# First attention of a streaming encoder step: stacked key and query parts for the scores

## The reference, cut to what matters

```python
k_sel = k_all[idx]; v_sel = v_all[idx]           # idx = top_k(indexer score)
logit = einsum('bqgrd,bqkgd->bqgrk', qg, k_sel) * HEAD_DIM ** -0.5
p = softmax(where(valid, logit, -inf))
o = einsum('bqgrk,bqkgd->bqgrd', p, v_sel)       # 16 query heads, 4 key heads, 64 wide
```

## Time and profile before

| | us |
|---|---|
| median of 3 runs | 1539.61 (1539.01 to 1540.18) |
| profiled execution, span from first to last instruction | 1537.2 |
| profiled execution, time of its own | not listed beside the span |
| first attention, from its first to its last turn of pairs | 183.2 to 281.8 |

### The profile page before, as it was taken

One profiled execution on the slowest core, in us unless ns is written; L12 is line 12 of the kernel. 1 busy time (PEld: TensorE's weight loads), 2 busy tenths in 40 slices (PEclk: granted clock), 3 DMA queues, 4 the chain that ended last, 5 costly groups with the idle time before them and its releaser, 6 DMA issues.

```text
span 1537.2 us, 29298 instructions
## 1 busy us (share of the span) xinstructions
PE 1496.9 (97%) x11509; PEld 1374.7 (89%) x11509; DVE 1057.4 (69%) x2025; ACT 634.3 (41%) x1265; POOL 580.0 (38%) x346
## 2 busy tenths in 40 slices
PE   5999999999999999999999999999999999999998
PEld 2768966899999999999888888887999999999998
DVE  1559866668887778877634444457997877688753
ACT  3434366444552145532533333335254541355423
POOL 1234841124662056642222222231227640366421
PEclk8999999999999999999999999999999999999999
DMA  9874510232244433443264444442542355343521
GB/s 333 269 264 150 140 37 2 72 108 69 83 129 141 156 89 104 121 141 99 51 191 127 127 126 126 126 127 71 168 120 56 83 160 184 83 110 83 152 83 62
DMA packets 244455, 189.23 MB, mean 123 GB/s; under 512 B 12888, under 2 KB 228608, under 8 KB 240112
## 3 DMA queue, kind: packets, MB, share of 16 engines
q1 hardware_dynamic: 231232, 178.61, 38.9%
q10 hardware_dynamic: 13104, 8.97, 1.8%
HBM read 175.44 MB, written 8.50 MB: 120 GB/s over the span
## 4 chain that ended last, share of the span: by engine, by line
PE 86%; DVE 5%; ACT 3%; issue 2%; DMA 2%; POOL 1%; SPq 0%; ACTq 0%; POOLq 0%; DVEq 0%
PE lin L858 40%; PE lin L1430 26%; PE lin L875 5%; PE S L1199 2%; PE O L993 1%; PE O L1321 1%; PE O L1252 1%; DVE acc_out L2644 1%; PE S L1274 1%; ACT act_hi L1655 1%; PE T L1232 1%; DMA ada_raw<-in_w_ada 1%; PE S L1118 1%; PE S L1062 1%; PE T L1289 1%
## 5 line engine op out<-in xcount | busy, mean ns | idle before, releaser
L2137 POOL TENSOR_TENSOR w_lo<-w_raw,w_hi 128x1024 fp32r<-128x1024 f32 (+3 forms) x68 | 168.2, 2475 | 407.7 <-ACT w_hi L1602 407.7
L2228 POOL TENSOR_TENSOR w_lo<-ada_raw,w_hi 128x512 fp32r<-128x512 f32 x114 | 156.5, 1375 | 242.8 <-ACT w_hi L1903 242.8
L1602 ACT ACTIVATE w_hi<-w_raw 128x1024 fp32r<-128x1024 f32 (+2 forms) x110 | 125.1, 1139 | 225.5 <-PE lin L858 212.3
L858 PE MATMUL lin<-act_hi,w_hi 128*128 128x288 f32 (+1 forms) x1088 | 164.6, 302 | 4.9 <-ACT act_hi L1634 2.0
L858 PE MATMUL lin<-act_hi,w_lo 128*128 128x288 f32 (+1 forms) x1088 | 167.3, 300 | 0.2
L858 PEld LDWEIGHTS lin<-act_hi,w_hi 128*128 128x128 f32 (+1 forms) x1088 | 149.5, 190 | 15.1 <-issue 10.3
L858 PE MATMUL lin<-act_lo,w_hi 128*128 128x288 f32 (+1 forms) x1088 | 162.1, 298 | 0.0
L858 PEld LDWEIGHTS lin<-act_hi,w_lo 128*128 128x128 f32 (+1 forms) x1088 | 150.0, 188 | 7.4 <-issue 6.7
L858 PEld LDWEIGHTS lin<-act_lo,w_hi 128*128 128x128 f32 (+1 forms) x1088 | 149.6, 188 | 3.4 <-issue 2.9
L2228 POOL TENSOR_TENSOR w_lo<-s_tmp,w_hi 128x512 fp32r<-128x512 f32 x76 | 129.2, 1718 | 15.0 <-ACT w_hi L1906 14.7
L1430 PE MATMUL lin<-act_hi,w_hi 128*128 128x288 f32 x608 | 105.5, 296 | 0.7 <-DVE Z L2801 0.7
(11 more groups left out here) (347 smaller groups left out, 3023.5 us busy)
## 6 DMA issues: line engine op xcount, KB each, us to landing
ada_raw<-in_w_ffn_in SPq DMA_DIRECT2D x76, 512.0 KB, 5.2
w_raw<-in_w_ffn_out SPq DMA_DIRECT2D x32, 704.0 KB, 5.0
ada_raw<-in_w_ada SPq DMA_DIRECT2D x20, 1024.0 KB, 7.8
ada_raw<-in_w_ada SPq DMA_DIRECT2D x32, 512.0 KB, 5.1
w_raw<-in_w_in_b SPq DMA_DIRECT2D x32, 512.0 KB, 4.2
w_raw<-in_w_in_a SPq DMA_DIRECT2D x16, 512.0 KB, 5.9
ada_qo<-in_w_ada SPq DMA_DIRECT2D x8, 1024.0 KB, 7.3
ada_raw<-in_w_ada_final SPq DMA_DIRECT2D x16, 512.0 KB, 5.6
```

What stands on the lines that cost most here:

```text
L858: last = nc.tensor.matmul(lin_u(u)[0:m, tok], w, (lo if p == 2 else hi)[:, at(t) if at else t, tok], start=(p == 0 and t == 0), stop=(p == ...
L1602: A(w_hi[:, u % 2, 0:n], w_raw[:, u % 2, 0:n], ACT.Copy).then_inc(whi_done, 1)
L2137: TT(w_lo[:, u % 2, 0:n], w_raw[:, u % 2, 0:n], w_hi[:, u % 2, 0:n].bitcast(F32), ALU.subtract)\
L2228: TT(ring(w_lo, q), raw, ring(w_hi, q).bitcast(F32), ALU.subtract).then_inc(ws_lo_p, 1)
```

## The change

Keys and queries of the first attention get a high and a low part in fp32r. `kT4` becomes fp32r and holds, for each key head, the high part on one half of the partitions and the low part on the other. The queries of a pair lie in `q_hi` (two buffers) and in `q_lo0` or `q_lo1`, for each head on all 128 partitions: both halves the same. A score is then two products of full height, `q_hi` and `q_lo` against the stacked key parts, added in PSUM. The samples of both heads lie side by side, so that one pair of products gives their scores and DVE takes their maximum in one operation. The score products of pair p read none of `qo`.

- ACT: `k_high` in place of `k_dup` (as many copies); `q_high`, three copies for each pair: pairs 0 and 1 between the projections' copies, pair p + 2 after the exponentials that ACT computes at k = 2 of pair p.
- POOL: `k_low` after `split_lo(U_V + 1)` and after `split_lo(U_Q + 2)`; `q_lows` of pairs 3 to 7 after `split_pair` of pairs 0 to 4.
- DVE: `q_lows` of pairs 0, 1 and 2, within the last top-k rounds, after the second `max_unit` and at n = 3; `cache_keys` makes both parts of the cached keys.
- SP: `q_double`, four DMAs for each pair, from the half of the partitions that has a head to the other half; pairs 2 to 7 stand in its queue one behind the other after the swap for the last queries, and the loads of the first sums come after them. `q_hi` and `q_lo0` share their place with `ada_raw`, whose first loads for sums therefore wait for the last score unit.
- PE: before the scores of a pair it waits for the four DMAs in place of the rotation.

```diff
+        q_hi = sb("q_hi", [P, 2, 2 * TOK], F32R, scope=s)
+        q_lo0 = sb("q_lo0", [P, 2 * TOK], F32R, scope=s)
...
-        kT4 = sb("kT4", [P, NG, NK], scope=a)
+        kT4 = sb("kT4", [P, NG, NK], F32R, scope=a)
...
+        Q_PARTS = [(0, 0, TOK, 0), (1, NP_, TOK, TOK), (1, 0, NP_, TOK + NS)]
+        def q_tile(e, k):
+            c = k * P if e == 0 else TOK + NS + k * P
+            return slice(c, c + P)
...
-                    sp.wait_ge(ada_used, 3 * KT)
+                    sp.wait_ge(s_done, 4 * PAIRS)
...
+            def q_double(pair):
+                sp.wait_ge(qhi_done, pair + 1)
+                sp.wait_ge(qlo_done, pair + 1)
+                for buf in (q_hi[:, pair % 2, :], q_low(pair)[:, :]):
+                    for e in range(2):
+                        own, other = slice(64 * e, 64 * e + 64), slice(64 - 64 * e, P - 64 * e)
+                        cols = slice(e * TOK, (e + 1) * TOK)
+                        sp.dma_start(buf[other, cols].bitcast(F32), buf[own, cols].bitcast(F32))\
+                          .then_inc(qdup_in[pair % 2], 16)
...
+                if j == 6:
+                    q_double(0)
...
+            def last_queries(m):
+                if m < 3:
+                    rope_swap(U_Q + PAIRS - 3 + m)
+                if m == 0:
+                    q_double(1)
+                if m == 2:
+                    for pair in range(2, PAIRS):
+                        q_double(pair)
...
-                    pe.wait_ge(rope_done, rope_of(U_Q + n // 4) + 1)
+                    pe.wait_ge(qdup_in[n // 4 % 2], 64 * (n // 8 + 1))
             def sa_unit(n):
                 k, pair, bank = n % 4, n // 4, (S, S2)[n % 2]
-                groups = [(0, P, k * P, 0, (k + 1) * P, 384 if k == 0 else 0)]
+                halves = (q_hi[:, pair % 2, :], q_low(pair)[:, :])
+                nk, col = (k + 1) * P, 384 if k == 0 else 0
+                for e in range(2):
+                    for j, q in enumerate(halves):
+                        last = nc.tensor.matmul(bank[:, e, col:col + nk], q[:, q_tile(e, k)],
+                                                kT4[:, pair // 2, 0:nk], start=(j == 0), stop=(j == 1))
                 if k == 0:
-                    groups.append((1, NS, NP_, NP_, PAST + NS, 0))
-                for sample, rows, tok, key, nk, col in groups:
-                    for e in range(2):
-                        r = slice(64 * e, 64 * e + 64)
-                        out = bank[64 * e:64 * e + 64] if sample else bank[0:P]
-                        last = nc.tensor.matmul(out[:, e, col:col + nk], qo[r, pair, tok:tok + rows],
-                                                kT4[r, pair // 2, key:key + nk],
-                                                start=True, stop=True)
+                    for j, q in enumerate(halves):
+                        last = nc.tensor.matmul(bank[:, 0, 0:PAST + NS], q[:, NP_:NP_ + 2 * NS],
+                                                kT4[:, pair // 2, NP_:NK], start=(j == 0), stop=(j == 1))
                 last.then_inc(s_done, 1)
...
-            pe.wait_ge(kdup_done, 2)
+            pe.wait_ge(khi_done, 8)
+            pe.wait_ge(klo_done, 4)
...
+            def k_high(j):
                 act.wait_ge(rope_done, rope_of(U_K + j) + 1)
-                for e in range(2):
-                    for half in range(2):
-                        for c0, c1, d0 in ((0, NP_, 0), (NP_, TOK, NP_ + PAST)):
-                            last = A(kT4[64 * half:64 * half + 64, 2 * j + e, d0:d0 + c1 - c0],
-                                     kR[64 * e:64 * e + 64, c0:c1], ACT.Copy)
-                last.then_inc(kdup_done, 1)
+                for e, half in ((0, 0), (0, 1), (1, 1), (1, 0)):
+                    for c0, c1, d0 in ((0, NP_, 0), (NP_, TOK, NP_ + PAST)):
+                        last = A(kT4[64 * half:64 * half + 64, 2 * j + e, d0:d0 + c1 - c0],
+                                 kR[64 * e:64 * e + 64, c0:c1], ACT.Copy)
+                    last.then_inc(khi_done, 1)
+            def q_high(pair):
+                act.wait_ge(rope_done, rope_of(U_Q + pair) + 1)
+                if pair == 0:
+                    act.wait_ge(ada_used, 3 * KT)
+                if pair >= 2:
+                    act.wait_ge(s_done, 4 * pair - 4)
+                for e, c0, c1, d0 in Q_PARTS:
+                    last = A(q_hi[64 * e:64 * e + 64, pair % 2, d0:d0 + c1 - c0], qo[64 * e:64 * e + 64, pair, c0:c1],
+                             ACT.Copy)
+                last.then_inc(qhi_done, 1)
...
+                if j == 4:
+                    q_high(0)
+                if j == 5:
+                    q_high(1)
...
+                if k == 2 and n // 4 + 2 < PAIRS:
+                    q_high(n // 4 + 2)
...
+            def k_low(j):
+                for e in range(2):
+                    pool.wait_ge(khi_done, 4 * j + 2 * e + 1)
+                    if e == 1:
+                        pool.wait_ge(klo_done, 2 * j + 1)
+                    own = slice(64 * e, 64 * e + 64)
+                    for c0, c1, d0 in ((0, NP_, 0), (NP_, TOK, NP_ + PAST)):
+                        part = kT4[own, 2 * j + e, d0:d0 + c1 - c0]
+                        last = TT(part, kR[own, c0:c1], part.bitcast(F32), ALU.subtract)
+                    last.then_inc(klo_done, 1)
+                pool.wait_ge(klo_done, 2 * j + 2)
...
             split_lo(U_V + 1, N)
+            k_low(0)
             rope(U_K + 1)
             split_lo(U_Q, N)
             split_lo(U_Q + 1, N)
             split_lo(U_Q + 2, N)
+            k_low(1)
...
+            def q_lows(pair):
+                pool.wait_ge(qhi_done, pair + 1)
+                pool.wait_ge(olo_done, pair - 2)
+                for e, c0, c1, d0 in Q_PARTS:
+                    own = slice(64 * e, 64 * e + 64)
+                    if d0 == TOK:
+                        pool.wait_ge(qlo_half, pair - 2)
+                    last = TT(q_low(pair)[own, d0:d0 + c1 - c0], qo[own, pair, c0:c1],
+                              q_hi[own, pair % 2, d0:d0 + c1 - c0].bitcast(F32), ALU.subtract)
+                    if e == 0:
+                        last.then_inc(qlo_half, 1)
+                last.then_inc(qlo_done, 1)
+                pool.wait_ge(qlo_done, pair + 1)
             rope(U_Q + PAIRS - 1)
             for pair in range(PAIRS - 1):
                 split_pair(pair)
+                if pair + 3 < PAIRS:
+                    q_lows(pair + 3)
...
-                V.tensor_copy(kT4[:, 2 * h:2 * h + 2, NP_:NP_ + PAST],
-                              T[:, :].rearrange("p (g c) -> p g c", g=2)).then_inc(t_free, 1)
+                both = T[0:64, :].rearrange("p (g c) -> p g c", g=2)
+                cols = slice(NP_, NP_ + PAST)
+                V.tensor_copy(kT4[0:64, 2 * h:2 * h + 2, cols], both).then_inc(kchi_done, 1)
+                dve.wait_ge(kchi_done, h + 1)
+                V.tensor_tensor(kT4[64:P, 2 * h:2 * h + 2, cols], both, kT4[0:64, 2 * h:2 * h + 2, cols].bitcast(F32),
+                                ALU.subtract).then_inc(t_free, 1)
...
+            def q_lows(pair):
+                dve.wait_ge(qhi_done, pair + 1)
+                for e, c0, c1, d0 in Q_PARTS:
+                    own = slice(64 * e, 64 * e + 64)
+                    last = V.tensor_tensor(q_low(pair)[own, d0:d0 + c1 - c0], qo[own, pair, c0:c1],
+                                           q_hi[own, pair % 2, d0:d0 + c1 - c0].bitcast(F32), ALU.subtract)
+                last.then_inc(qlo_done, 1)
...
+                if it == 3:
+                    q_lows(0)
...
+                if k == 0 and bias_s is None:
+                    one(ps[:, :], bank[:, 0, 0:PAST + NS], sc[:, SOFF:], negmax[:, 0, 2:3])
+                elif k == 0:
...
+            q_lows(1)
...
+                if n == 3:
+                    q_lows(2)
```

35 lines of the change are left out of this document (20 added, 15 removed).

## The result

| | before | after |
|---|---|---|
| median, us | 1539.72 (4 runs beside the changed kernel's) | 1557.95 (1556.52 to 1559.16, 4 runs) |
| profiled span, us | 1537.2 | 1554.7 |
| mean granted clock of TensorE | 0.995 | 0.988 |

The ratio is 1.0119, 95% interval 1.0107 to 1.0131: slower, as forecast, but by 18.2 us and not by 5. The page's busy line after, beside the earlier trace rows: PE is busy 5 us longer, POOL 25 us, ACT 12 us, DVE 11 us.

What follows compares the result with a forecast made beforehand. TensorE, busy in 97% of the span, was taken as the bound. +0.7 to pair 2's scores, +5.0 for five turns and -0.7 at the end gave +5.0: 1537.2 + 5.0 + 2.4 = 1544.6 us, 8-in-10 range 1536.5 to 1549.

Steps and rivals of the forecast that it cites:

- The loop: First attention, pairs 3 to 7: query copies, subtractions, DMAs make a turn 13.15 us against 12.16, +5.0 us over five.
- Rival A: Same loop: POOL's 64-row operations cost half, loop 11.65 us, total 1536.1 us; chance 0.2.
- Rival B: Same loop: wait nearly hidden, loop 12.2 to 12.7 us, total +0 to +3, say 1541; chance 0.2.
- Three of 0.75, 0.2 and 0.68: Pair 2's query subtractions on DVE, behind its last copy of pair 0: prices in us of the three operations.
- DVE and POOL at work together: Upper bound on the price of POOL's 64-row operations in the loop, put at +0.5.
- Pair 1's parts are ready just in time: Before the loop: pair 1's query parts arrive when its scores need them, no cost counted.
- +0.7 up to pair 2's scores: Before the loop: pair 2's k=0 scores start about 0.7 us later than before; bounds -0.6 to +1.8.
- The score units: PE's score products in each turn: k=0 to 3 take 0.74, 0.47, 0.69, 0.91 us against 1.11, 0.63, 0.84, 1.06.
- Rival C: Score units: narrow fp32r products run at the old rate, k=0 takes 1.2 us, 3.7 more, total 1548.3; chance 0.1.
- If nothing else waited, a turn would be 11.5 us: Attention turn set by PE alone: 12.16 less 0.68 us saved in score units.
- the forecast's -0.7: After the five turns: the last pair's shorter score units save 0.37 + 0.16 + 0.15 us.
- The prologue's lateness: Stage before the attention: POOL's new key subtractions make PE 1.3 us late; bounds 0 and 2.5.

Runs made afterwards that it cites:

- e9: Changed kernel with e7's edit, ScalarE's copies of the high query parts in two halves, the first head's one iteration earlier, GpSimd starting on it at once: 1541.58 us.
- e13: e9 with SyncE sending each half across as soon as made, and pair 3's low parts ahead of GpSimd's first output split: 1540.73 us.
- e4: Changed kernel with VectorE's subtractions for the low query parts of pairs 1 and 2 replaced by zero fills: 1549.24 us.
- e7: Changed kernel with the low query parts of pairs 1 and 2 made on GpSimd too, no work left out: 1551.53 us.
- e3: Changed kernel with six added 512-column products on TensorE ahead of the wait for duplicated queries, pairs 3 to 7: 1554.71 us.
- e2: Changed kernel with ScalarE making the high parts of the pair after next one iteration earlier (k=1, not k=2): 1551.07 us.
- e6: Changed kernel with the low query parts of the last five pairs made on VectorE too, instead of GpSimd: 1550.53 us.
- e11: Changed kernel with query parts of pairs 2 to 7 neither made nor copied across the rows, only the full-height products left: 1544.69 us.
- e14: e13 with the second key head's low parts made by GpSimd after pair 0's output split instead of before the ropes: 1544.95 us.
- e16: e14 with pair 0's four copies across the rows issued by ScalarE instead of SyncE: 1542.54 us.
- e5: Changed kernel with the second key head's high and low parts made earlier on ScalarE and GpSimd: 1562.04 us.

## Why the forecast was right in sign and wrong in size

**The loop, right.** "The sum 13.15 us" measured 13.27, with the links in the order forecast: ACT's copies 1.35 to 1.45 (1.42), POOL 3.05 (3.0), landing 2.45 us from the last issue (2.1, from the earlier trace rows). PE stood 1.24 to 1.28 us in four of the five turns and 0.82 in one, not 1.6. Five regular turns would have cost 5.5 us against 5.0. The estimate of 2.34 us for the landing, from the fit of the Trainium skill (DMA: Bandwidth & Descriptors, Anatomy of one DMA) for transfers issued by GpSimd, was nearer to the 2.45 measured for SP's than the 2.1 that I took from transfers of half the size. Rival A is out: POOL took 1412 ns for 64 x 576, what it took for 128 x 576 in the earlier trace rows. Rival B's half-hidden wait and its 1541 us are what e9 and e13 reached by reordering, not the change itself.

**The step that failed: DVE's subtractions.** "Three of 0.75, 0.2 and 0.68", 1.6 us a pair, with "DVE and POOL at work together" bounded at +0.5, and for pair 1 no cost at all ("Pair 1's parts are ready just in time"), where PE then stood longest, 2.81 us. The bound came from no row. Measured beside POOL: 3.82, 5.59 and 3.66 us; alone: 1.58. The forecast had +0.7 up to pair 2's scores, the run +8.3; e4 and e7 give 5.8 to 6.9 us of S(2) back by taking DVE's subtractions away. POOL was full at the first two pairs' places (14.84 of 15 us between 170 and 185 us in the kernel before, 13.2 of 13.4 between pair 0's and pair 1's scores), so there the collision was to be expected in full, and in part at pair 2's, where POOL had 8.6 of 12.2 us. The Trainium skill states the rule (SBUF — State Buffer, Who interferes with whom): "A DVE instruction with two SBUF inputs contends with a GpSimd instruction that reads SBUF", the second to issue being blocked until the first has finished. The trace agrees in kind: 6.07 us for three instructions against POOL operations of 1.4 to 2.4 us. By that rule each of nine instructions may wait a whole POOL operation, 1.4 to 2.4 us, and not the 0.17 that a bound of +0.5 for three comes to.

**What was not in the forecast: the clock.** The forecast priced each wait at its own length. After three of seven waits of 0.8 to 2.8 us TensorE's granted clock was 0.50, for 3.4 to 6.8 us, and a turn took 15.2 or 15.35 instead of 13.27 us: 4.0 us in the loop, where e3 shows that filled gaps bring all turns to 13.35, and some 3 us more, by the estimate under e4, in the 8.3 us before it. So about 7 of the 17.3 us are the clock, a term that the forecast did not have at all; the two falls behind DVE's waits make 3.0 and 1.9 of them (e4, without these waits, has none), the one in the loop 2.1. Not each wait has this: in e4 five waits of 1.27 us passed at 1.00, in e2 and e6 one of 2.81. What decides it is open here. It goes with the spread of one kernel's runs: of e4's, the one of 1546.4 us has a mean clock of 0.994 and the one of 1551.7 us 0.987.

**The score units, wrong with little consequence for the sum.** Forecast 0.74, 0.47, 0.69 and 0.91 us. From a unit's start to that of the next group, e13 has 1.26 with the stand (1.01 without), 0.81, 0.92 and 1.04; the kernel before had 1.26, 0.81, 0.92 and 1.06. The distances between the later products of a unit are what the line through the earlier trace rows gives, 0.12 at 256 and 0.17 at 384 columns, but the first product of each unit takes 0.17 to 0.34 us. Rival C's narrow products are out: four of 128 columns start 0.11 us apart. "If nothing else waited, a turn would be 11.5 us" comes near what PE does behind a wait (11.58), but in a dense loop something else does wait: e11 measures 12.19. The change had nothing to win there. The last turn's -0.6 us against the forecast's -0.7 is therefore luck: it came from the wait in front of it, and in e13, without that wait, the last turn takes 12.17.

**The prologue's lateness, nearly right.** 1.8 us against 1.3, which was put down to POOL's key subtractions; e14 gives 1.8 back by moving them.

**What stays open.** Which idle stretches are followed by a fall of the clock, and whether the first score unit can be brought back to 183.2 us without one of the losses of e14 to e16. A third buffer for the high parts was not tried.

## What to carry to other kernels

Before an engine is given an operation with two SBUF inputs, look at what VectorE's and GpSimd's other one does in that very stretch; where it runs such operations back to back, the price is theirs and not the operation's own, and everything written behind it on its queue, a small operation or another queue's weight load, is late by as much. A wait on TensorE is to be priced with the clock that may follow it, here 2 us behind some waits of 1.3. And before a unit of work is made shorter, look at what starts after it: if that waits for another engine's chain, a faster unit turns into idle time, which one run without the new work's other costs (e11) shows at once.

## What the runs showed of the hardware that I had not expected

- Three VectorE subtractions (64 rows; 576, 64 and 512 columns) take 1.58 us while GpSimd stands and 3.33 (e5) to 6.07 us (e16) beside its two-input operations, of which some grow from 1.4 to 1.9 us.
- The granted clock stood at 0.50 for 3.4 to 10.2 us (10.2 in e3) behind some waits of TensorE of 1.3 to 3.8 us, and did not fall behind others of the same length.
- Six added products of 512 columns in each of five idle stretches made the kernel 3.2 us faster.
- GpSimd's subtraction takes 1.41 us for 576 columns on 64 rows and on 128.
- An SBUF-to-SBUF copy of 64 x 576 fp32 numbers, issued by SyncE, landed 2.43 to 2.46 us after the last of four issues in the loop; one issued by ScalarE before the loop (e16) took 3.93 us.
- The first product of a full-height fp32r unit takes 0.17 (128 columns) to 0.34 us (512) to the start of the second; the others follow at 0.11 to 0.23 us.
